# Sparse attention and a recurrence on one TensorE: the attention moved from three array shapes into 64x64 corners

## The reference

```python
s_c = einsum(qb, kc) * scale;  p_c = masked_softmax(s_c, cmp_end <= t)     # 63 compressed keys
s_s = einsum(qb, ks) * scale;  p_s = masked_softmax(s_s, pos_s <= t)       # selected blocks: here all up to t
s_w = einsum(qb, kw) * scale;  p_w = masked_softmax(s_w, 0 <= t - pos_w < 512)
out = g[0] * (p_c @ vc) + g[1] * (p_s @ vs) + g[2] * (p_w @ vw)            # gates per token and head
```

## Time and profile before

| | |
|---|---|
| time, median of 3 runs | 2514.84 us (2512.34 to 2515.33) |
| span of the profiled execution | 2509.2 us |
| own time of the profiled execution | not given; the median lies 5.6 us above the span |
| PE busy | 2471.1 us, 98% |
| DVE busy | 1723.1 us, 69% |
| ACT busy | 1052.3 us, 42% |
| attention and recurrence | from 1066 to 1520 us of the span |

### The profile page before, as it was taken

How to read it: one execution, slowest core, us unless ns; L and a number is a source line. 1 busy time by engine, 2 the same in 40 slices (tenths; PEclk the granted TensorE clock), 3 DMA queues, 4 the chain that set the end, 5 groups by cost and what they waited for, 6 DMA issues and landing times. The chain is left out here.

```text
span 2509.2 us, 47304 instructions
## 1 busy us (share of the span) xinstructions
PE 2471.1 (98%) x19440; PEld 2024.9 (81%) x19440; DVE 1723.1 (69%) x2720; ACT 1052.3 (42%) x1827; POOL 94.9 (4%) x146
## 2 busy tenths in 40 slices
PE   8999999999999999999999999999999999999999
PEld 7888888888887778977888787877788888888887
DVE  6976676688655464589888788634468776676676
ACT  4322223345443343466655564523343322223443
POOL 0000000000000000021231110000000000000000
PEclk9999999999999999999999999999999999999999
DMA  4223323654442258932211116501222413326464
GB/s 152 96 89 121 120 73 121 239 185 150 130 136 64 96 175 253 258 95 53 53 46 44 45 45 221 178 21 34 68 76 87 136 67 121 118 74 218 139 200 148
DMA packets 279268, 297.78 MB, mean 119 GB/s; under 512 B 75442, under 2 KB 209712, under 8 KB 279088
## 3 DMA queue, kind: packets, MB, share of 16 engines
q1 hardware_dynamic: 278080, 294.29, 37.4%
q10 hardware_dynamic: 1008, 0.92, 0.1%
HBM read 208.54 MB, written 81.36 MB: 116 GB/s over the span
## 5 line engine op out<-in xcount | busy, mean ns | idle before, releaser
L1246 PE MATMUL f_ps<-hi,f_wh 128*128 128x512 f32 x656 | 255.6, 390 | 0.8 <-DVE f_wl L930 0.8
L1248 PE MATMUL f_ps<-hi,f_wl 128*128 128x512 f32 x656 | 255.2, 389 | 0.0
L2859 PE MATMUL f_ps<-hi,f_ahead_h 128*128 128x512 f32 x384 | 160.0, 417 | 0.8 <-PEq L72 0.8
L1246 PE MATMUL f_ps<-f_t3h,f_t2h 128*128 128x512 f32 x392 | 152.5, 389 | 0.0
L1247 PE MATMUL f_ps<-f_t3l,f_t2h 128*128 128x512 f32 x392 | 152.5, 389 | 0.0
L1248 PE MATMUL f_ps<-f_t3h,f_t2l 128*128 128x512 f32 x392 | 152.5, 389 | 0.0
L2861 PE MATMUL f_ps<-hi,f_ahead_l 128*128 128x512 f32 x384 | 149.9, 390 | 0.0
L2860 PE MATMUL f_ps<-one_lo,f_ahead_h 128*128 128x512 f32 x384 | 149.8, 390 | 0.0
L1246 PEld LDWEIGHTS f_ps<-hi,f_wh 128*128 128x128 f32 x656 | 123.1, 188 | 27.2 <-issue 1.6
L1248 PEld LDWEIGHTS f_ps<-hi,f_wl 128*128 128x128 f32 x656 | 123.1, 188 | 25.6
L1247 PE MATMUL f_ps<-one_lo,f_wh 128*128 128x512 f32 x344 | 133.8, 389 | 0.0
(11 more groups left out here) (636 smaller groups left out, 6609.9 us busy)
## 6 DMA issues: line engine op xcount, KB each, us to landing
act<-one_y SPq DMA_DIRECT2D x30, 512.0 KB, 3.6
f_work<-act SPq DMA_DIRECT2D x30, 512.0 KB, 3.5
act<-y SPq DMA_DIRECT2D x30, 512.0 KB, 3.6
arena<-act SPq DMA_DIRECT2D x30, 512.0 KB, 3.7
one_y<-in_w_in SPq DMA_DIRECT2D x25, 512.0 KB, 4.0
early<-in_ffn_w_gate SPq DMA_DIRECT2D x11, 1024.0 KB, 6.2
early<-in_ffn_w_up SPq DMA_DIRECT2D x11, 1024.0 KB, 8.7
f_raw<-in_ffn_w_gate SPq DMA_DIRECT2D x10, 1024.0 KB, 6.3
```

The lines of the kernel that those rows point to most:

```text
L1246: nc.tensor.matmul(out, wh, xh, start=start, stop=False)
L1248: return nc.tensor.matmul(out, wl, xh, start=False, stop=stop)
L2859: nc.tensor.matmul(dense_ps[:, b, cols], w_hi[:, b, k, :], hi[:, k, cols], start=(k == 0), stop=False)
```

## The change

Everything that PE does for the attention is done in 64x64 corners.

- Scores: a step is now 64 queries of two heads instead of 128 queries of one. Keys are fp32 and stored by parity of their block of 64: even blocks in rows 0 to 63, odd ones in rows 64 to 127. Four fp32 products, one to a corner, give one step.
- `scale` is gone. A 64x64 diagonal matrix with gate over denominator (`diag`) is made on DVE, one for a step with selected keys, two for one with window and compressed keys.
- `bank` and `values` become one event, `turn(n)`: each 64x64 block of probabilities is the stationary operand and the diagonal the moving one, which transposes and scales it, in the two corners off the diagonal; between these products stand those of fill `n-1` with the values, in the other two corners. A fill has up to 8 such blocks; blocks wholly in the future or outside the window are no longer turned. There are 136 fills.
- Values lie in both halves of the partitions, loaded twice. `finish` only copies; POOL squares.
- Rotated queries and keys are stored once, in fp32: no high and low part. Queries are loaded half as often, keys in runs of 64 elements.

```diff
-                        nc.tensor.matmul(at, q[:, ring, 0, head % 4, :], keys, start=True, stop=False)
-                        mm = nc.tensor.matmul(at, q[:, ring, 1, head % 4, :], keys, start=False, stop=True)
+                at, m = span(s)
+                for r, c in CORNERS:
+                    mm = nc.tensor.matmul(s_ps[rows(c), r, 0:m * CH], query(r, c), keys[k // 2][rows(r), g, at * CH:(at + m) * CH], start=True, stop=True)
+                if k >= 2:
+                    for c in range(2):
+                        mm = nc.tensor.matmul(s_ps[rows(c), 0, HALF - CH:HALF], query(0, c), kc[rows(0), g, :], start=True, stop=True)
...
-                for m, (br, blk, col) in enumerate(turns(u)[f]):
-                    for h in range(2):
-                        src = (sel if br == 1 else win)[:, u % 2, h, col:col + P]
-                        mm = nc.tensor.transpose(t_ps[:, 2 * m + h, :], src, ident[:])
...
+                def probs(br, half, col, x):
+                    src = (sel if br == 1 else win)[:, u % 2, half]
+                    for a_ in range(2):
+                        mm = nc.tensor.matmul(t_ps[rows(1 - a_), x, :], src[rows(a_), col:col + CH], diag[rows(a_), u % 2, half, br, :],
+                                              start=True, stop=True)
+                    return mm
...
+                    cols, n_cols = halves[0][0] * CH, len(halves) * CH
+                    for r in range(2):
+                        mm = nc.tensor.matmul(o_ps[rows(r), 0, cols:cols + n_cols], val[rows(r)],
+                                              probT[rows(r), (n - 1) % 2, x:x + len(halves)].rearrange("p x q -> p (x q)"),
+                                              start=(fv == 0 and x == 0), stop=(br == 0))
...
+                while given < len(ahead) or taken < len(before):
+                    if given < len(ahead) and (taken == len(before) or given <= before[taken][3]):
+                        mm = probs(*ahead[given])
...
+                    else:
+                        mm = values(*before[taken])
...
-                nc.vector.tensor_tensor(coef[:, s % 8, of], rden[:, s % 8, of], gate_of, ALU.mult).then_inc(weighted, 1)
...
-                nc.vector.tensor_scalar(slot[:, 0:cols], slot[:, 0:cols], coef[:, s % 8, 1:2], None, ALU.mult).then_inc(scaled, 1)
...
+                for br in (1,) if k < 2 else (2, 0):
+                    unit = eye_ok if i == half == br == 0 else eye
+                    by = rden[:, s % 8, (br != 0):(br != 0) + 1]
+                    nc.vector.tensor_scalar(diag[:, u % 2, half, br, :], unit[:], by, gate_rows[:, i, half, pair, br:br + 1],
+                                            ALU.mult, ALU.mult).then_inc(weighted, 1)
...
-        return e[0] == "values" and "columns" or e[0] == "rw" and (e[2] != "var" or not crossed(e[1])) and "corners" or "whole"
+        return "whole" if e[0] == "tile" or e[0] == "rw" and e[2] == "var" and crossed(e[1]) else "corners"
...
-                    nc.vector.tensor_tensor(r_lo[:, n % 2, :].bitcast(F32R), home(at[("rot", n)]), r_hi[:, n % 2, :], ALU.subtract).then_inc(lo_rotated, 1)
+                    nc.vector.tensor_tensor(turned[:, n % 4, :], x, xs[:, n % 2, :], ALU.add).then_inc(rotated, 1)
```

More of the change, by code:

```diff
@@ L1448, in shape_tables @@
     neg = np.float32(-1e30)
-    zero = np.zeros((P, T - P), np.float32)
-    tok = np.arange(T).reshape(TT, P)
-    cmp_ok = (np.arange(NB) * 16 + 31)[None, None, :] <= tok.T[:, :, None]
+    t, key = t[:, None] % CH, np.arange(CH)[None, :]
+    zero, dead = np.zeros((P, CH), np.float32), np.full((P, CH), neg, np.float32)
+    future, past = (np.where(late, neg, np.float32(0)) for late in (key > t, key <= t))
+    cmp_ok = (np.arange(NB) * 16 + 31)[None, None, :] <= t[:, :, None] + CH * np.arange(2 * TT)[None, :, None]
     return {
@@ L1476, with span, key_columns, packed @@
 NB = 63
-CMP_COL = 5 * P
+CMP_COL = 10 * CH
 LEVELS = 5
 UNITS = TT * PAIRS
-def key_blocks(u):
[L1484 to L1487, removed]
+def span(s):
+    x = 2 * (s // 4 // PAIRS) + s % 2
+    at = max(0, x - 8) // 2 if s % 4 >= 2 else 0
+    return at, x // 2 + 1 - at
+def key_columns(s):
+    x, (at, m) = 2 * (s // 4 // PAIRS) + s % 2, span(s)
+    return {b: (b % 2 * m + b // 2 - at) * CH for b in range(max(0, x - 8) if s % 4 >= 2 else 0, x + 1)}
+def key_blocks(u):
+    found = []
+    for br in (1, 2):
+        halves = [key_columns(4 * u + 2 * br - 2 + half) for half in range(2)]
+        blocks = [(br, b, [(half, halves[half][b]) for half in range(2) if b in halves[half]]) for b in sorted(halves[0] | halves[1])]
+        found += sorted(blocks, key=lambda x: len(x[2]), reverse=br == 1)
+    return found + [(0, 0, [(half, CMP_COL) for half in range(2)])]
+def packed(blocks, most):
+    fills, used = [[]], 0
+    for br, b, halves in blocks:
+        if used + len(halves) > most:
+            fills.append([])
+            used = 0
+        fills[-1].append((br, b, halves, used))
+        used += len(halves)
+    return fills
+def width(fill):
+    return sum(len(halves) for _, _, halves, _ in fill)
 def turns(u):
     blocks = key_blocks(u)
-    return [blocks[m:m + 2] for m in range(0, len(blocks), 2)]
+    return min((packed(blocks, most) for most in range(2, 9)), key=len)
 FILLS = [(u, f) for u in range(UNITS) for f in range(len(turns(u)))]
@@ L1518, in last_step @@
 def last_step(u, f):
-    return 4 * u + (1 if all(br == 1 for br, _, _ in turns(u)[f]) else 3)
+    return 4 * u + (1 if all(x[0] == 1 for x in turns(u)[f]) else 3)
+CORNERS = ((0, 0), (1, 1), (0, 1), (1, 0))
 STAY = 10.0
@@ L1590, in joint_plan @@
[L1590 to L1604, removed]
+        u, m, extra = s // 4, span(s)[1], 0.2 * (s % 4 >= 2)
@@ new lines, in joint_plan @@
+        us = 0.001 * CH * len(key_columns(s))
+        event(("score", s), "pe", 0.11 * m + 0.03 + 0.5 * extra, s and ("max", s - 1))
+        event(("max", s), "dve", 0.3 + 0.14 * m + extra, ("score", s), u >= 2 and ("turn", FIRST_FILL[u - 1] - 1))
+        event(("exp", s), "act", 0.4 + us + 2 * extra, ("max", s), s and ("exp", s - 1))
+        event(("diag", s), "dve", 0.35 + extra, ("exp", s), s and ("diag", s - 1))
+    for n in range(len(FILLS) + 1):
+        before = turns(FILLS[n - 1][0])[FILLS[n - 1][1]] if n else []
+        fill = turns(FILLS[n][0])[FILLS[n][1]] if n < len(FILLS) else []
+        last = n and FILLS[n - 1]
+        event(("turn", n), "pe", 0.11 * max(width(fill), width(before)), fill and ("diag", last_step(*FILLS[n])), n and ("copy", n - 1),
+              n and last[1] == 0 and last[0] and ("finish", last[0] - 1))
+        if fill:
+            event(("copy", n), "act" if n % 2 else "dve", 0.13 + 0.066 * width(fill), ("turn", n))
@@ new lines, in joint_plan @@
+    for u in range(UNITS):
+        i, n = u // PAIRS, FIRST_FILL[u + 1]
+        if u % PAIRS == 0 and i:
+            event(("tile", i - 1), "pe", 0.25, ("fold", u - 1), ("turn", n))
+        event(("finish", u), "act", 0.35, ("turn", n), u % PAIRS == 0 and i and ("tile", i - 1))
+        event(("fold", u), "pool", 0.4 if u % PAIRS == 0 else 0.8, ("finish", u), u and ("fold", u - 1))
+    event(("tile", TT - 1), "pe", 0.25, ("fold", UNITS - 1))
+    for i in range(TT):
+        event(("tile_ms", i), "act", 0.3, ("tile", i))
+        event(("tile_inv", i), "dve", 0.9, ("tile_ms", i))
+        if i + 1 < TT:
+            needs["turn", FIRST_FILL[PAIRS * (i + 1) + 1] + 1].append(("tile_ms", i))
@@ L1749, in attend_and_recur @@
     with core.stage() as ctx:
-        ks, kw = hi[:, 0:2, :], hi[:, 2:4, :]
+        keys = [keys_of(hi, branch) for branch in range(2)]
+        vs = [hi[:, at, col:col + P].bitcast(F32) for at, col in VALUES_AT]
         q = queries_of(hi)
@@ L1973, in turn_probs, with turn @@
+                if k >= 2:
+                    for c in range(2):
+                        mm = nc.tensor.matmul(s_ps[rows(c), 0, HALF - CH:HALF], query(0, c), kc[rows(0), g, :], start=True, stop=True)
+                mm.then_inc(scored, 1)
+            def turn(n):
+                now = before = []
+                if n < len(FILLS):
+                    u, f = FILLS[n]
+                    now = turns(u)[f]
+                    pe.wait_ge(weighted, steps_through(last_step(u, f)))
                 if n:
+                    v, fv = FILLS[n - 1]
+                    before = turns(v)[fv]
@@ new lines, in values @@
+                def values(br, blk, halves, x):
+                    g = v % PAIRS // 2
+                    val = vc[:, rows(g)] if br == 0 else (vs[blk] if br == 1 else vw[:, blk])[:, rows(g)]
+                    cols, n_cols = halves[0][0] * CH, len(halves) * CH
+                    for r in range(2):
+                        mm = nc.tensor.matmul(o_ps[rows(r), 0, cols:cols + n_cols], val[rows(r)],
+                                              probT[rows(r), (n - 1) % 2, x:x + len(halves)].rearrange("p x q -> p (x q)"),
```

(39 more changed lines are left out.)

307 lines of the change are left out of this document (136 added, 171 removed).

## The result

| | before | after |
|---|---|---|
| median | 2513.59 us (2510.27 to 2515.33, 4 runs) | 2555.07 us (2551.87 to 2557.33, 4 runs) |
| ratio, 95% interval | | 1.0168 [1.0153, 1.0182] |
| span of the profiled execution | 2509.2 us | 2549.8 us |

The forecast was 2436 us, the range 2405 to 2480. The kernel became 1.7% slower.

The account below looks back on a forecast made before the run. The prediction took PE to bound the attention stage, a quarter of its time being changes of shape. -454 + 374 + 1 = -79 on a span of 2509.2 gave 2430, plus 5.6 for the runs' median: 2436 us, range 2405 to 2480.

Parts of the forecast that it names:

- a floor per instruction: Rival: in the attention stage no MATMUL starts sooner than 25 ns after the last; stage 413 us, total 2474; chance 0.05.
- 142 + 69 + 128 + 4 + 6 = 349: PE's attention work in us: recurrence, scores, turning with values, the rest, changes of shape; 349 against 454 before.
- PE idle over 50 us in the stage: Sign that would show the forecast wrong: PE idle for more than 50 us in the attention stage.
- Changes of shape: PE in the attention: from 529 to at most 32 changes at 0.19 us each, 6 us against 101, so -95.
- Scores -9: Score products on PE, four to a step in the corners: 69 us against 78.
- turning and values -1: Turning probabilities and multiplying values on PE, overlapped in the corners: 128 us against 60 + 69.
- corners abreast: Corner products on PE run side by side: eight-block fills 0.94 us apart; 1.5 us and more would show otherwise.
- the rival of row halves that run one after the other: Row halves writing one PSUM bank run in sequence, doubling scores and turning: stage 572 us, total 2633; chance 0.03.
- 374 with waits: Forecast length of the attention stage: PE's work of 349 us plus 25 us of waits.
- forecast 313: DVE's busy time in the attention stage falls from 379 to about 313 us, with diagonals at 0.25 to 0.35.
- The chains: Turning, score-to-maximum and recurrence chains in the attention, each at 70% of the new stage, add 25 us of waits.
- The edges: More value loads at the stage's start cost 0 to 5 us, taken as 1; preparation, covered by PE, taken as 0.

Follow-up runs that it names:

- the first streak: Kernel of its own, TensorE alone: 1536 fp32 products of 64 columns in 64x64 corners, no waits; 28.8 ns per MATMUL with gaps, 30.4 over the whole.
- the last: Same kernel of its own, final part: 1536 products of 64 columns again while SP moves 24 loads of 1 MB; 39.2 ns per MATMUL beside transfers, 28.3 after.
- the alone-standing price: Kernel of its own, TensorE alone: corner and whole-array products in turn, then sorted; 1.65 against 1.31 us a period, one change of shape 0.17 us.
- one constant: Kernel before with the planner counting 0.5 us instead of 0.1 us for a change of shape: 2565.24 us, ratio 1.0214.

## Why the prediction was wrong

- **The step that failed** is the supply of instructions, a term that the sum put at nothing. The rival "a floor per instruction", which comes nearest to it, got 0.05, with the words "eighty instructions in 1.17 us, 14.6 ns each, speak against; only a much longer streak could differ". The longest burst of before that I read was eighty MATMULs; a block has 128. Inside a block the 14.6 ns are right: the first streak has 14.7. The limit is on blocks, and before's trace hardly touched it, with blocks 5.59 us apart. The sum "142 + 69 + 128 + 4 + 6 = 349" priced array time alone and never asked what 15,500 MATMULs need: at the streak's 28.8 ns between gaps they need 447 us, at its mean of 30.4 472, at the stage's own 3.97 us a block 484, and 489.5 were measured. Even that rival was sized too low, at 25 ns and 413 us with waits. One of the signs of being wrong came, "PE idle over 50 us in the stage": 103.
- The Trainium skill has the two rules that bear on it. "TensorE: Matmul & The Clock Gate" (section "Wait — 56ns, not 53.3ns?") gives a floor of 25 ns from start to start however few the columns; the bursts here go below it, at 14.6 and 14.7 ns, and the mean over blocks lies above it. "Runtime: NRT & Kernel Launch" (section "Instruction fetch mechanics") says that instructions are refilled in blocks of 256 and that crossing into the next is mostly hidden. The size agrees with the 16384 bytes and 128 pairs seen here; that it is hidden doesn't hold for these products, which lose 1.64 us of 3.73 at each block in the streak.
- **Changes of shape**, "-95": right. They went from 529 to 31 by the written order, and the alone-standing price is 0.17 us.
- **Scores -9, turning and values -1, corners abreast**: the prices stand. PE's busy time fell by 56 us. An event of eight blocks with the values of another eight takes 0.94 us, as forecast:

```profile
1211.37 0.27 PE L2054 MATMUL ar_t_ps<-ar_diag,ar_sel 64*64 64x64 f32 x2
...
1212.31 0.65 PE L2028 MATMUL ar_s_ps<-hi 64*64 64x256 f32 x8
```

  In it both row halves write to one bank of PSUM, by the code. So the rival of row halves that run one after the other, 1.9 us for such an event, did not come. (The streak is no test of it, as its row halves write to different banks.)
- **The sum without the gaps.** The starts on PE that lie over 0.5 us after the one before add up to 129 us in 121 gaps; 489.5 - 129 is 360, against 349 of work. (PE's busy time is 386, since an instruction counts as open for 0.22 us or more though the next starts 15 ns after it: before each gap that adds some 0.2 us, 25 us in all, an estimate.) 87 of these gaps, 100 us, end with "issue"; without them alone the stage would take some 389 us, an estimate, against 374 with waits.
- **DVE**: forecast 313, measured 325. The diagonals took longer than taken, 365 instead of 310 ns. PE's idle time that ends with DVE is 17 us, 9 more than before.

```profile
L2354 DVE TENSOR_SCALAR ar_diag<-ahead_eye,ar_rden,ar_gate_rows 128x64 f32<-128x64 f32 x188 | 63.5, 365 | 4.7
```

- **The chains**, 25 us of waits: PE's idle time that ends with DVE or ACT is 22 us. That is near, but no test, since the instructions came first and could hide more. Where turning products are left out, they show: 411 us where blocks alone would take 373.
- **The edges**: taken as +1 in the stage and nothing ahead of it; the stage starts 4.6 us later. PE's cover, which I had named, has holes now. Stretches of the preparation after, of which before had 50.00 and 39.62 us busy:

```profile
900.00:950.00 50.00, 47.99 (x205) 35.62 (x204) 31.14 (x26) 24.94 (x31) 0.00 (x0) 1.00 0.53 166
...
1000.00:1040.00 40.00, 37.93 (x239) 34.64 (x238) 21.02 (x19) 13.17 (x18) 0.00 (x0) 0.96 1.04 239
```

  There PE had three more gaps: 1.2 and 0.9 us at 916 and 918, which end with ACT, and 2.0 us at 1034.76, which ends with DVE's `f_ahead_l`. They make 4.0 of the 4.6 us. Why these events are late was not tested; the order of events in the preparation was planned anew.

What stays open: why a block takes 3.7 us when its transfer takes 0.9 to 1.5. In the changed stage PE restarts about 1.4 us after a block has landed, and the next one's transfer begins about 1.4 us after that. With the transfer that is 3.8 us, near the median of 3.87: a round in which each part waits for the one before. What sets the two parts of 1.4 us no experiment changes.

By these numbers a gain is there to be had, though no run with the right output shows it: 498 changes of shape are gone, 85 us at 0.17, and 91 us more of idle time took their place. The two kernels below the time of before compute something else: one leaves turning products out, the other turns by the keys in place of the diagonal.

## What to carry to other kernels

Count instructions as well as columns. Divide the MATMULs of a stage by 128 and multiply by 3.7 to 4 us; if that exceeds the array's work, narrower products cost time however well they fill the array, and in such a stage merging two products into one with twice the columns gains while halving columns gains nothing. A price per instruction read off a burst holds only as far as the burst: look for the longest streak that the new kernel will have, and at the queue "instruction" in the profile, whose packets per microsecond show how near the limit a stage is (5.59 us a block before, with room for 40% more). And a change in an order written by a planner is an edit of its own: one constant cost more here than the whole change.

## What the hardware showed that was not expected

- TensorE's instructions arrive in blocks of 128 MATMULs with their weight loads, one in 3.73 us at 64 fp32 columns in corners; 3.58 us is the shortest mean pace seen (768 products of 128 columns, 1536 MATMULs, in 42.96 us).
- Beside some 330 GB/s of transfers a MATMUL takes over a third longer: 39.2 ns against 28.3 after them, in part at half the clock.
- The granted clock kept its upper level (2.4 GHz) beside gaps of 1.6 to 2.4 us, in the first streak from 21.5 us on and in the last from 257. It fell to the lower one (1.2 GHz) at 11.3, within the gap of 6.6 us, and six times from 192.2 on, the first time right after one of 4.3 us. The page's row has it in 40 slices of 7.3 us:

```profile
PEclk9759999999999999999999999967687575989999
```

- A transposition of 128x128 takes 109 ns in a row of 1536 (167.6 us), one MATMUL each; four took 0.41 us in the earlier trace rows.
